# One-hot rows of the gate stage: two VectorE instructions of 512 elements for four tokens in place of four of 128

## The chip, the core and the metric

The kernel runs on 1 core of one Trainium2 chip. The metric is the device time of one execution in microseconds (us), as the median of several runs.

## What is computed

One inference step of a two-layer decoder trunk: 256 prompt tokens and 8 sequences of 4 new tokens, 288 tokens in all, width 1024. Each layer has a mixer (retention with a short convolution in layer 0, HGRN2 in layer 1) and then a PEER channel mixer, which is where the change lies:

```
q = (hb @ wq).reshape(T, PEER_HEADS, 2, PEER_DK // 2)
s = jnp.einsum('thpc,hpkc->thpk', q, keys)
v1, i1 = lax.top_k(s[:, :, 0], PEER_TOPK)
v2, i2 = lax.top_k(s[:, :, 1], PEER_TOPK)
...
eid = e1 * N_KEYS + e2
gate = jax.nn.softmax(vals, axis=-1)
act = jax.nn.gelu(jnp.einsum('thkd,td->thk', u[eid], hb))
w = (gate * act)
return jnp.einsum('thk,thkd->td', w, v[eid])
```

Each token has 8 heads with 16 picks each, 128 picks in all, and each pick names one of 128 x 128 experts by a first index e1 and a second index e2, with a softmax gate. All is float32.

## The kernel before

The kernel doesn't gather experts. For each layer it multiplies all 288 tokens with all 16384 rows of u (section "u0" or "u1", each 128 blocks of 512 KB), keeps the gelu of the products in SBUF (`gates`, 128 partitions x 128 x 288), multiplies that by the gate of each expert, zero for those not picked, and multiplies the result with all rows of v (section "v0" or "v1"). These weight products are split in three passes (lines 1184 to 1186) of a rounded part and its rest, made by ScalarE (line 422) and VectorE (line 660).

Between u and v lies the gate stage, in which the 128 x 128 gate matrix of each token is built as a matrix product over the token's 128 picks. `choice[:, 0, t]` holds the first index of each pick of token t (picks on the partitions), `choice[:, 1, t]` the second one, `choice[:, 2, t]` the gate. For a token, the one-hot row of each pick's first index, scaled by its gate, is one 128 x 128 operand (`onehot`), the one-hot row of its second index the other (`seconds`). Their product over the picks is the gate matrix. Tokens go in groups of four, 6 groups in a turn of the loop (TOKENS = 24), 12 turns and 72 groups in a layer. In each turn:

- VectorE (`weigh`, line 1080) has `firsts` (line 1085), which makes the scaled one-hot rows of a group's tokens, one tensor_scalar a token with compare and multiply (line 1090), into a ring of 8 slots; and `apply` (line 1093), which multiplies the gelus of a group by its gate matrices from PSUM (line 1096). The order written out is firsts 0, firsts 1, apply 0, firsts 2, apply 1, ... firsts 5, apply 4, apply 5, and then the next turn. `firsts` waits until the product that last read the slot is done (`onehot_free`, which TensorE raises for each token), `apply` until its group's four products are done.
- GpSimd (line 367) makes iota minus the second index for a group, 128 x 512, as soon as the slot of two groups before has been read out by ScalarE.
- ScalarE squares it (line 528) and turns it into the one-hot `seconds` by relu(1 - square) (line 531), which waits until the products of two groups before are done.
- TensorE (lines 1399 to 1412) makes the four products of a group into one of two PSUM banks (line 1409). It waits for the bank (`gate_free`, raised by `apply`), for the group's `seconds` (`second_ready`) and, for each token by itself, for its row (`first_ready`). A product of float32 operands is two passes in the profile, so a group has 8.

In layer 0 the loop carries more work: each turn begins with the conditioning products of layer 1 (line 1212, 16 passes of 512 columns), whose weights the SP queue loads into the four `raw` slots; after groups 1 and 3 TensorE turns a part of the result (line 1239), which ScalarE copies before and after (lines 470 and 477), in its own order between the lines 528 and 531.

The order of work on an engine is the order written; nothing is planned at run time.

Of the kernel before, what the change touches and what calls it, by code (L numbers as in the profile page):

```python
# [27 lines left out]
ALU = mybir.AluOpType  # L28
# [3 lines left out]
P = 128  # L32
# [5 lines left out]
T = T_PROMPT + T_SAMPLE  # L38
# [33 lines left out]
TOKENS = 24  # L72
# [29 lines left out]
def trunk(nc, t):  # L102

    with ExitStack() as ctx:
        def sb(name, shape, dt=F32):
            return ctx.enter_context(nc.sbuf_tensor(name, shape, dt))

        def sem(name):
            return ctx.enter_context(nc.semaphore(name))
# [7 lines left out]
        choice = sb("choice", [P, 3, T])  # L117
        onehot = sb("onehot", [P, 8, P])
        ident = sb("ident", [P, P])
        ones = sb("ones", [P, P])  # L120
        iota = sb("iota", [P, P])
# [137 lines left out]
        mixer_done, keys_landed = sem("mixer_done"), sem("keys_landed")  # L259
        x_spilled, x_back = sem("x_spilled"), sem("x_back")  # L260
        exped, picks_ready = sem("exped"), sem("picks_ready")
        first_ready, second_ready = sem("first_ready"), sem("second_ready")
        onehot_free = sem("onehot_free")
        apart_ready, apart_squared = sem("apart_ready"), sem("apart_squared")
        gate_free = sem("gate_free")
# [369 lines left out]
        def _(dve):  # L635
# [444 lines left out]
            def weigh(l):  # L1080

                if l == 0:
                    dve.sem_inc(gate_free, 2)

                def firsts(i, g):

                    for j in range(4):
                        tok = i * TOKENS + (4 * g + j)
                        dve.wait_ge(onehot_free, tok + (T * l + 1))
                        dve.tensor_scalar(onehot[:, (4 * g + j) % 8, :], iota[:], choice[:, 0, bass.ds(tok, 1)], choice[:, 2, bass.ds(tok, 1)],  # L1090
                                          ALU.is_equal, ALU.mult).then_inc(first_ready, 1)

                def apply(i, g):
                    dve.wait_ge(onehot_free, i * TOKENS + (T * l + 4 * g + 4 + 8))
                    w = gates[:, :, bass.ds(i * TOKENS + 4 * g, 4)]
                    dve.tensor_tensor(w, w, ps[:, 6 + g % 2, :].rearrange("p (j e) -> p e j", j=4), ALU.mult).then_inc(gate_free, 1)  # L1096
                with dve.Fori(0, T // TOKENS) as i:
                    firsts(i, 0)
                    for g in range(1, TOKENS // 4):
                        firsts(i, g)  # L1100
                        apply(i, g - 1)
                    apply(i, TOKENS // 4 - 1)
                dve.wait_ge(gate_free, (T // 4) * (l + 1) + 2)
                dve.sem_inc(w_ready, T // 4)  # L1104

# [65 lines left out]
        def _(pe):  # L1171
# [195 lines left out]
            def peer(l):  # L1367
# [12 lines left out]
                for j in range(LISTS):  # L1380
                    g, lo = 32 * (j // 4), (j % 4) * P
# [17 lines left out]
                with pe.Fori(0, T // TOKENS) as i:  # L1399
                    if l == 0:  # L1400
                        pe.wait_ge(ada_row, i * 2 + 24)
                        condition(ps[0:NS, 0, :], i + FIRST["ada1"] // 4)
                    for g in range(TOKENS // 4):
                        pe.wait_ge(gate_free, i * (TOKENS // 4) + ((T // 4) * l + g + 1))
                        for j in range(4):
                            pe.wait_ge(first_ready, i * TOKENS + (T * l + 4 * g + j + 1))
                            if j == 0:
                                pe.wait_ge(second_ready, i * (TOKENS // 4) + (T // 4 * l + g + 1 + 2))
                            pe.matmul(ps[:, 6 + g % 2, j * P:j * P + P], onehot[:, (4 * g + j) % 8, :], seconds[:, g % 2, j, :].bitcast(F32),  # L1409
                                      start=True, stop=True).then_inc(onehot_free, 1)  # L1410
                        if l == 0 and g in (1, 3):
                            turn(i + 12, g // 2)
# [147 lines left out]
```

## Time and profile before

| | us |
|---|---|
| median of 3 runs | 2921.13 (2918.17 to 2921.57) |
| the profiled execution, its span from first to last instruction | 2932.5 |
| TensorE busy in it | 2684.2 |
| VectorE busy in it | 1793.5 |
| ScalarE busy in it | 1351.1 |
| GpSimd busy in it | 181.9 |

The profile is of one execution; the page gives its span and no other time of its own. PE is TensorE's products, PEld its weight loads, DVE VectorE, ACT ScalarE, POOL GpSimd; a name with q (DVEq) is the engine's queue of instructions. Busy time counts an instruction from its start to its end, a hold by another engine included. In a timeline, "x8" means that eight like instructions were merged into one line, and the bracket gives the idle time of the engine before the line and what ended it. PEclk is the mean granted TensorE clock as a share of 2.4 GHz; its two levels are 2.4 and 1.2 GHz.

### The profile page before, as it was taken

What the parts mean: (1) busy time and instruction counts of PE and PEld (TensorE: products, weight loads), DVE (VectorE), ACT (ScalarE), POOL (GpSimd) and SP (SyncE); (2) the same over time, 40 slices, a digit from 0 to 9 for tenths busy, and PEclk for the clock granted to TensorE, in tenths of its full rate; (3) what the DMA queues carried; (4) which work ended last, traced back from release to release, by engine and by line L of the source; (5) the groups of instructions that cost most, each with busy time, mean ns of one, the idle gap of its engine ahead of it and who ended that gap; (6) DMA issues with size and microseconds to landing.
All of it is one profiled execution on the core that took longest, in us unless ns stands there. A gap on an engine that the chain in (4) does not pass through costs nothing.

```text
span 2932.5 us, 55686 instructions
## 1 busy us (share of the span) xinstructions
PE 2684.2 (92%) x17972; PEld 2441.2 (83%) x17972; DVE 1793.5 (61%) x4076; ACT 1351.1 (46%) x2491; POOL 181.9 (6%) x200
## 2 busy tenths in 40 slices
PE   7997899999989899999979796999999866999997
PEld 3962799999955579999979685899999855999996
DVE  2424568884466755555554877589854599555554
ACT  2501345556543445555545323355556544455553
POOL 1000000000022310000000000000000144000000
PEclk8987899999998989999989788899999978999998
DMA  6544444545533335555534112345445300555552
GB/s 231 165 130 161 132 137 158 168 148 163 162 124 100 100 127 182 164 165 164 165 120 162 37 57 102 122 151 161 154 158 165 122 0 0 167 165 165 165 165 86
DMA packets 108380, 401.03 MB, mean 137 GB/s; under 512 B 12352, under 2 KB 12496, under 8 KB 107168
## 3 DMA queue, kind: packets, MB, share of 16 engines
q1 hardware_dynamic: 103104, 375.44, 39.7%
q0 software_dynamic: 5216, 24.87, 2.3%
q8 instruction: 29, 0.48, 0.1%
q14 instruction: 31, 0.25, 0.0%
HBM read 389.60 MB, written 10.65 MB: 136 GB/s over the span
## 4 chain that ended last, share of the span: by engine, by line
PE 81%; DVE 12%; issue 3%; ACT 2%; DMA 1%; DVEq 1%; ACTq 0%; POOL 0%; SPq 0%; POOLq 0%
PE ps L1184 21%; PE ps L1186 21%; PE ps L1185 21%; PE ps L1212 6%; PE ps L1409 4%; DVE onehot L1090 2%; DVE spl L660 1%; PE ps L1329 1%; PE ps L1345 1%; DVE big L1096 1%; PE ps L1358 1%; DMA raw<-in_ada_w 1%; PE ps L1248 1%; DVE big L1041 1%; DVE big L1036 1%
## 5 line engine op out<-in xcount | busy, mean ns | idle before, releaser
L1184 PE MATMUL ps<-hs,spl 128*128 128x288 f32 x4960 | 1481.8, 299 | 75.9 <-DVE hs L712 46.0
L1185 PE MATMUL ps<-hs,spl 128*128 128x288 f32 x4960 | 1473.0, 297 | 0.0
L1186 PE MATMUL ps<-hs,spl 128*128 128x288 f32 x4960 | 1470.5, 296 | 0.0
L660 DVE TENSOR_TENSOR spl<-raw,spl 128x512 fp32r<-128x512 f32 x1240 | 844.4, 692 | 844.9 <-ACT spl L422 842.6
L422 ACT ACTIVATE spl<-raw 128x512 fp32r<-128x512 f32 x1240 | 774.4, 631 | 628.6 <-PE ps L1186 628.2
L1184 PEld LDWEIGHTS ps<-hs,spl 128*128 128x128 f32 x4960 | 940.1, 190 | 89.5 <-issue 58.2
L1186 PEld LDWEIGHTS ps<-hs,spl 128*128 128x128 f32 x4960 | 943.0, 190 | 0.0
L1185 PEld LDWEIGHTS ps<-hs,spl 128*128 128x128 f32 x4960 | 941.7, 190 | 0.0
L1409 PE MATMUL ps<-hs,onehot 128*128 128x128 f32 x1152 | 222.7, 346 | 81.0 <-DVE onehot L1090 56.5
L1409 PEld LDWEIGHTS ps<-hs,onehot 128*128 128x128 f32 x1152 | 185.0, 239 | 121.3 <-issue 56.8
L1090 DVE TENSOR_SCALAR onehot<-iota,choice 128x128 f32<-128x128 f32 x576 | 239.2, 480 | 5.5 <-PEq L1398 4.4
L367 POOL TENSOR_TENSOR hs<-iota,choice 128x512 fp32r<-128x512 f32 x144 | 152.3, 1058 | 1245.7 <-ACT big L517 1002.5
L1212 PE MATMUL ps<-raw,cs 128*10 128x512 f32 x384 | 184.5, 636 | 13.6 <-ACT cs L554 6.7
L517 ACT ACTIVATE big<-ps 128x288 f32 (+1 forms) x256 | 105.6, 412 | 177.9 <-PE ps L1186 177.2
L1212 PEld LDWEIGHTS ps<-raw,cs 128*10 128x10 f32 x384 | 34.7, 96 | 147.2 <-issue 128.5
L1096 DVE TENSOR_TENSOR big<-big,ps 128x512 f32 x144 | 98.0, 681 | 86.7 <-PE ps L1409 85.7
L531 ACT ACTIVATE hs<-hs 128x512 fp32r<-128x512 f32 x144 | 91.0, 632 | 86.6 <-PE ps L1409 78.0
L1123 DVE TENSOR_TENSOR hs<-big,hs 128x288 fp32r<-128x288 f32 x256 | 115.8, 452 | 0.6 <-ACT hs L541 0.6
L541 ACT ACTIVATE hs<-big 128x288 fp32r (+1 forms) x256 | 109.9, 429 | 5.5 <-DVEq L1104 5.5
L517 ACT ACT_TABLE_LOAD x62 | 79.5, 1283 | 63.1 <-PE ps L1186 63.1
L528 ACT ACTIVATE hs<-hs 128x512 fp32r<-128x512 f32 x144 | 88.7, 616 | 3.2 <-POOL hs L367 3.1
L484 ACT ACTIVATE big<-ps 128x288 f32 (+1 forms) x92 | 37.9, 412 | 95.8 <-PE ps L1186 95.7
(222 smaller groups left out, 1292.3 us busy)
## 6 DMA issues: line engine op xcount, KB each, us to landing
raw<-in_peer_u SPq DMA_DIRECT2D x256, 512.0 KB, 3.4
raw<-in_peer_v SPq DMA_DIRECT2D x256, 512.0 KB, 3.4
raw<-in_ada_w SPq DMA_DIRECT2D x96, 512.0 KB, 4.3
raw<-in_peer_wq SPq DMA_DIRECT2D x32, 512.0 KB, 3.3
raw<-in_hg_w_in SPq DMA_DIRECT2D x32, 512.0 KB, 3.4
raw<-in_ab_w_in SPq DMA_DIRECT2D x28, 512.0 KB, 3.4
raw<-in_ab_w_out SPq DMA_DIRECT2D x8, 512.0 KB, 3.9
big<-in_state_hgrn POOLq DMA_DIRECT2D x8, 512.0 KB, 3.9
```

The source lines that it names most:

```text
L367: pool.tensor_tensor(apart[:, g % 2], iota[:, None, :].broadcast_to([P, 4, P]), choice[:, 1, bass.ds(i * TOKENS + 4 * g, 4)][:, :, None].b ...
L422: act.activation(spl[:, slot % 2, 0, cols], raw[:, slot, cols], ACT.Copy).then_inc(high_ready, 1)
L517: act.activation(gates[:, bass.ds(i * 4 + s, 1), :], ps[:, s % 2:s % 2 + 1, 0:T], ACT.Gelu).then_inc(gelu_ready, 1)
L660: dve.tensor_tensor(spl[:, slot % 2, 1, cols], raw[:, slot, cols], spl[:, slot % 2, 0, cols].bitcast(F32), ALU.subtract).then_inc(low_read ...
L1090: dve.tensor_scalar(onehot[:, (4 * g + j) % 8, :], iota[:], choice[:, 0, bass.ds(tok, 1)], choice[:, 2, bass.ds(tok, 1)], ALU.is_equal, AL ...
L1096: dve.tensor_tensor(w, w, ps[:, 6 + g % 2, :].rearrange("p (j e) -> p e j", j=4), ALU.mult).then_inc(gate_free, 1)
L1123: dve.tensor_tensor(hs[:, 1, slot, :], gates[:, bass.ds(e, 1), :].rearrange("p a t -> p (a t)"), hs[:, 0, slot, :].bitcast(F32), ALU.subtr ...
L1184: pe.matmul(out, spl[:, slot, 0, cols], high, start=start, stop=False, skip_group_check=True)
L1185: pe.matmul(out, spl[:, slot, 0, cols], low, start=False, stop=False, skip_group_check=True)
L1186: return pe.matmul(out, spl[:, slot, 1, cols], high, start=False, stop=stop, skip_group_check=True)
L1212: ins = pe.matmul(out, cs[:, k, :], raw[:, k // 2, ROWS * (k % 2):ROWS * (k % 2) + ROWS], start=k == 0, stop=k == KC - 1)
L1409: pe.matmul(ps[:, 6 + g % 2, j * P:j * P + P], onehot[:, (4 * g + j) % 8, :], seconds[:, g % 2, j, :].bitcast(F32), start=True, stop=True) ...
```

## The change

`firsts` is replaced by two functions. `mark` compares iota with the first indices of four tokens, broadcast to 128 x 4 x 128, in one tensor_tensor of 512 elements a partition, and raises a new semaphore `first_marked`. `scale` waits for that and multiplies the four rows in place by the four tokens' gates, also broadcast, in a second tensor_tensor, and raises `first_ready` once for the group. TensorE waits for `first_ready` once for each group, ahead of its first token. `mark` waits until all four slots are free.

The order on VectorE is changed too. A step of group g is scale g, apply g - 1, mark g + 1. At the end of a turn the order is scale 5, apply 4, mark and scale of the next turn's group 0, apply 5, mark of the next turn's group 1. For this the first turn's beginning and the last turn's end are written out, and the loop runs 11 times over what lies between.

```diff
--- before.py
+++ after.py
@@ -259,7 +259,7 @@
         mixer_done, keys_landed = sem("mixer_done"), sem("keys_landed")
         x_spilled, x_back = sem("x_spilled"), sem("x_back")
         exped, picks_ready = sem("exped"), sem("picks_ready")
-        first_ready, second_ready = sem("first_ready"), sem("second_ready")
+        first_marked, first_ready, second_ready = sem("first_marked"), sem("first_ready"), sem("second_ready")
         onehot_free = sem("onehot_free")
         apart_ready, apart_squared = sem("apart_ready"), sem("apart_squared")
         gate_free = sem("gate_free")
@@ -1082,24 +1082,51 @@
                 if l == 0:
                     dve.sem_inc(gate_free, 2)
 
-                def firsts(i, g):
-
-                    for j in range(4):
-                        tok = i * TOKENS + (4 * g + j)
-                        dve.wait_ge(onehot_free, tok + (T * l + 1))
-                        dve.tensor_scalar(onehot[:, (4 * g + j) % 8, :], iota[:], choice[:, 0, bass.ds(tok, 1)], choice[:, 2, bass.ds(tok, 1)],
-                                          ALU.is_equal, ALU.mult).then_inc(first_ready, 1)
+                groups = TOKENS // 4
+
+                def four(g):
+                    return onehot[:, 4 * (g % 2):4 * (g % 2) + 4, :]
+
+                def mark(i, g):
+
+                    dve.wait_ge(onehot_free, i * TOKENS + (T * l + 4 * g + 4))
+                    dve.tensor_tensor(four(g), iota[:, None, :].broadcast_to([P, 4, P]),
+                                      choice[:, 0, bass.ds(i * TOKENS + 4 * g, 4)][:, :, None].broadcast_to([P, 4, P]),
+                                      ALU.is_equal).then_inc(first_marked, 1)
+
+                def scale(i, g):
+
+                    dve.wait_ge(first_marked, i * groups + (T // 4 * l + g + 1))
+                    dve.tensor_tensor(four(g), four(g),
+                                      choice[:, 2, bass.ds(i * TOKENS + 4 * g, 4)][:, :, None].broadcast_to([P, 4, P]),
+                                      ALU.mult).then_inc(first_ready, 1)
 
                 def apply(i, g):
                     dve.wait_ge(onehot_free, i * TOKENS + (T * l + 4 * g + 4 + 8))
                     w = gates[:, :, bass.ds(i * TOKENS + 4 * g, 4)]
                     dve.tensor_tensor(w, w, ps[:, 6 + g % 2, :].rearrange("p (j e) -> p e j", j=4), ALU.mult).then_inc(gate_free, 1)
-                with dve.Fori(0, T // TOKENS) as i:
-                    firsts(i, 0)
-                    for g in range(1, TOKENS // 4):
-                        firsts(i, g)
+
+                def step(i, g, more=True):
+                    scale(i, g)
+                    if g:
                         apply(i, g - 1)
-                    apply(i, TOKENS // 4 - 1)
+                    if more:
+                        mark(i, g + 1)
+                last = T // TOKENS - 1
+                mark(0, 0)
+                for g in range(groups - 1):
+                    step(0, g)
+                with dve.Fori(0, last) as i:
+                    scale(i, groups - 1)
+                    apply(i, groups - 2)
+                    mark(i + 1, 0)
+                    scale(i + 1, 0)
+                    apply(i, groups - 1)
+                    mark(i + 1, 1)
+                    for g in range(1, groups - 1):
+                        step(i + 1, g)
+                step(last, groups - 1, more=False)
+                apply(last, groups - 1)
                 dve.wait_ge(gate_free, (T // 4) * (l + 1) + 2)
                 dve.sem_inc(w_ready, T // 4)
 
@@ -1403,8 +1430,8 @@
                     for g in range(TOKENS // 4):
                         pe.wait_ge(gate_free, i * (TOKENS // 4) + ((T // 4) * l + g + 1))
                         for j in range(4):
-                            pe.wait_ge(first_ready, i * TOKENS + (T * l + 4 * g + j + 1))
                             if j == 0:
+                                pe.wait_ge(first_ready, i * (TOKENS // 4) + (T // 4 * l + g + 1))
                                 pe.wait_ge(second_ready, i * (TOKENS // 4) + (T // 4 * l + g + 1 + 2))
                             pe.matmul(ps[:, 6 + g % 2, j * P:j * P + P], onehot[:, (4 * g + j) % 8, :], seconds[:, g % 2, j, :].bitcast(F32),
                                       start=True, stop=True).then_inc(onehot_free, 1)
```

## Rows read from the trace of the kernel before

**Rows 1.** The page: engines' busy time, and the chain that ended last.

```profile
PE 2684.2 (92%) x17972; PEld 2441.2 (83%) x17972; DVE 1793.5 (61%) x4076; ACT 1351.1 (46%) x2491; POOL 181.9 (6%) x200
...
PE 81%; DVE 12%; issue 3%; ACT 2%; DMA 1%; DVEq 1%; ACTq 0%; POOL 0%; SPq 0%; POOLq 0%
PE ps L1184 21%; PE ps L1186 21%; PE ps L1185 21%; PE ps L1212 6%; PE ps L1409 4%; DVE onehot L1090 2%; DVE spl L660 1%; PE ps L1329 1%; PE ps L1345 1%; DVE big L1096 1%; PE ps L1358 1%; DMA raw<-in_ada_w 1%; PE ps L1248 1%; DVE big L1041 1%; DVE big L1036 1%
```

**Rows 2.** Busy us by stretch, gate stages: PE, PEld, DVE, ACT, POOL, clock, DMA, GB/s.

```profile
824.40:1062.80 238.40, 210.88 (x857) 119.82 (x858) 158.35 (x359) 103.12 (x217) 75.42 (x72) 0.87 0.32 106
2325.90:2492.40 166.50, 112.92 (x576) 96.39 (x576) 161.24 (x360) 83.44 (x144) 76.92 (x72) 0.79 0.00 1
```

**Rows 3.** Groups of instructions, layer 1's gate stage: busy us, mean ns, idle before.

```profile
L1090 DVE TENSOR_SCALAR onehot<-iota,choice 128x128 f32<-128x128 f32 x288 | 120.9, 484 | 1.1 <-ACT big L517 1.1
...
L367 POOL TENSOR_TENSOR hs<-iota,choice 128x512 fp32r<-128x512 f32 x72 | 76.9, 1069 | 585.5 <-ACT big L517 501.4 <-ACT hs L531 84.0
L1096 DVE TENSOR_TENSOR big<-big,ps 128x512 f32 x72 | 49.0, 680 | 5.3 <-PE ps L1409 4.5
```

**Rows 4.** Timeline, the last groups of layer 1, where GpSimd is done.

```profile
2487.17 1.18 PE L1409 MATMUL ps<-hs,onehot 128*128 128x128 f32 x8 [0.39 <-DVE onehot L1090]
...
2488.39 0.63 ACT L531 ACTIVATE hs<-hs 128x512 fp32r<-128x512 f32 x1 [0.42 <-PE ps L1409]
...
2489.34 0.68 DVE L1096 TENSOR_TENSOR big<-big,ps 128x512 f32 x1
2489.94 1.11 DVE L1090 TENSOR_SCALAR onehot<-iota,choice 128x128 f32<-128x128 f32 x4
...
2490.42 1.18 PE L1409 MATMUL ps<-hs,onehot 128*128 128x128 f32 x8 [0.44 <-DVE onehot L1090]
2490.97 1.44 DVE L1096 TENSOR_TENSOR big<-big,ps 128x512 f32 x2
```

**Rows 5.** Timeline, a loop turn's start in layer 1: start, us, engine, line.

```profile
2453.63 2.98 DVE L1090 TENSOR_SCALAR onehot<-iota,choice 128x128 f32<-128x128 f32 x8
2453.70 1.04 POOL L367 TENSOR_TENSOR hs<-iota,choice 128x512 fp32r<-128x512 f32 x1 [1.47 <-ACT hs L531]
...
2454.95 4.74 PE L1409 MATMUL ps<-hs,onehot 128*128 128x128 f32 x24 [2.10 <-DVE onehot L1090]
2456.59 0.63 ACT L531 ACTIVATE hs<-hs 128x512 fp32r<-128x512 f32 x1 [2.54 <-PE ps L1409]
...
2457.28 1.83 DVE L1090 TENSOR_SCALAR onehot<-iota,choice 128x128 f32<-128x128 f32 x4
2457.39 1.13 POOL L367 TENSOR_TENSOR hs<-iota,choice 128x512 fp32r<-128x512 f32 x1 [2.65 <-ACT hs L531]
```

**Rows 6.** Groups by shape, whole span: VectorE tensor_tensor with both inputs in SBUF.

```profile
L660 DVE TENSOR_TENSOR spl<-raw,spl 128x512 fp32r<-128x512 f32 x1240 | 844.4, 692 | 844.9 <-ACT spl L422 842.6
...
L1036 DVE TENSOR_TENSOR big<-big,iota 128x2048 f32<-128x2048 f32 x8 | 18.3, 2289 | 0.1
```

**Rows 7.** Timeline, VectorE: a wait on the instruction right ahead.

```profile
731.80 0.57 DVE L1057 TENSOR_REDUCE small<-rstd 128x8 f32<-128x128 f32 x3
732.40 0.30 DVE L1060 RECIPROCAL small<-small 128x8 f32<-128x8 f32 x3
```

**Rows 8.** Timeline, TensorE in a turn of layer 0: conditioning, groups 0 and 5.

```profile
844.53 7.03 PE L1212 MATMUL ps<-raw,cs 128*10 128x512 f32 x16
851.49 1.16 PE L1409 MATMUL ps<-hs,onehot 128*128 128x128 f32 x8
...
861.74 2.10 PE L1409 MATMUL ps<-hs,onehot 128*128 128x128 f32 x8 [0.56 <-DVE onehot L1090]
```

**Rows 9.** Timeline, VectorE in the same turn: groups 2 and 5.

```profile
853.38 2.67 DVE L1090 TENSOR_SCALAR onehot<-iota,choice 128x128 f32<-128x128 f32 x4
...
861.16 1.83 DVE L1090 TENSOR_SCALAR onehot<-iota,choice 128x128 f32<-128x128 f32 x4
```

## The prediction

> **What bounds the kernel now.** I read the page first: TensorE is busy 92% of the span and the chain that ended last is 81% TensorE, but nearly all of that belongs to the weight products of lines 1184 to 1186 [rows 1]. The gate building of the change is elsewhere: two stretches, the gate stage of layer 0 (238.4 us) and of layer 1 (166.5 us), found by asking when line 1090 runs and then tabulating those stretches [rows 2]. Only they can move. In layer 1 VectorE is busy 161.2 of 166.5 us while TensorE has 112.9: VectorE sets the pace. In layer 0 TensorE is busy 210.9 of 238.4 us, because it also does the conditioning products.
>
> The groups of layer 1 show why VectorE is full [rows 3]: 288 row makers (line 1090) take 484 ns on average, although four with nothing in their way take 1.11 us together, 0.34 for one and a pitch of (1.11 - 0.34) / 3 = 0.257 [rows 4]. The timeline shows the rest [rows 5]. A row maker starts at 2453.63, GpSimd's line 367 at 2453.70; TensorE gets its first row only at 2454.95. A product starts 0.14 after its row is done (2489.94 + 0.34 to 2490.42 [rows 4]), so that row ended at 2454.81, 0.07 after GpSimd's end at 2454.74, and 0.84 late. At 2457.28 the row maker came first by more, and GpSimd took 1.13 in place of 1.04. So the two hold each other off. The product of VectorE with gates (line 1096) runs beside GpSimd unharmed at 680 ns mean [rows 3]; one of its inputs is in PSUM. Besides, at each turn of the loop TensorE stands for 2.10 us [rows 5]: the last product, the last line 1096, then a held row maker, one after the other.
>
> **The change, part by part.** A group is four tokens; a layer has 72, so before costs 166.5 / 72 = 2.31 us each in layer 1.
>
> *Instructions.* Four row makers per group go (4 x 0.257 = 1.03 us of pitch unheld). Two 512-element tensor_tensors come. A 512-element one takes 0.692, a 2048-element one 2.289, both from SBUF [rows 6]: 1.04 ns an element, 0.53 us of streaming and 0.16 around it. I take 0.68 for each, of which 0.12 lies ahead of the streaming and 0.04 behind. When nothing is awaited the next starts 0.60 after (2489.34 to 2489.94 [rows 4]). So VectorE gets more work, not less.
>
> *The new wait.* The scaling waits for the marking right ahead of it on the same engine. Nearest row: a semaphored pair, 731.80 + 0.57 to 732.40 [rows 7], 0.03 after the end; I take 0.04, so 0.72 from one start to the other. Queued behind it are the scaling, line 1096 and the next marking.
>
> *The hand-over.* TensorE now waits for a group's four rows together rather than for each. Its 8 passes take 1.16 at full clock [rows 8] and start 0.14 after the scaling ends.
>
> *The loop's turn.* The marks and scalings of the next turn go ahead of the last line 1096, so the 2.10 us stop goes; what is late next is VectorE's chain below. The first and last turns written out cost instructions only; I cost them at nothing, since VectorE's queue runs ahead of its work; without that cover each turn would pay some queue operations. No DMA is moved and no queue but VectorE's and TensorE's waits changes.
>
> *Does GpSimd hold off the new instructions?* No row shows a tensor_tensor with both inputs in SBUF beside GpSimd. Bounds: never held, as line 1096; or held whole, as line 1090. I take held: the new ones read everything from SBUF, where line 367 reads too, and the row that escapes has an input in PSUM. The Trainium skill (SBUF — State Buffer, section "Who interferes with whom") says that a VectorE instruction with two SBUF inputs contends with a GpSimd instruction that reads SBUF, which speaks against this change. By it the sum below holds; without it the first rival does; no run here shows it yet.
>
> *Sum for layer 1.* I follow one group round. Scaling ends; 0.14; TensorE 1.16; ScalarE's line 531 starts 0.04 later (2487.17 + 1.18 to 2488.39 [rows 4]); GpSimd starts 0.80 after that (2456.59 to 2457.39 [rows 5]); it holds the inputs from about 0.12 for 0.88 (its 1.04 less the same 0.16). Meanwhile line 1096 runs hidden. Marking was issued but is held, streams 0.53, 0.04 to its end, 0.04 wait, 0.12, scaling streams 0.53, 0.04. Sum 0.14 + 1.16 + 0.04 + 0.80 + 0.12 + 0.88 + 1.30 = 4.44 for two groups, since GpSimd works two ahead: **2.22 a group**. At half clock TensorE's 8 passes take 2.10 [rows 8], and the round gives 2.69; where the marking gets in ahead of GpSimd it is about 2.53; I take 2.60. The mean granted clock in this stage was 0.79 [rows 2], so 42% of the time at 1.2 GHz. The long stops after which it stood at half are gone, but no row shows this new rhythm. Ends: none at half, or 42% again; I take the middle, 21%: 2.30. 71 x 2.30 = 163.3, plus a head of 2.5 (GpSimd 1.04, two activations of 0.63, hand-overs) and a tail of 2.1 (0.14 + 1.16 + 0.13 + 0.68, the 0.13 being 2490.42 + 1.18 to the second line 1096 at 2491.73 [rows 4]): 167.9, or **+1.4**. Ends: 162.2 (-4.3) with none, 173.6 (+7.1) with 42%.
>
> *Sum for layer 0.* Each of 12 turns begins with 7.03 us of conditioning products [rows 8], which hide the first two groups before and after: the loop's turn gains nothing. Groups 2 to 5 took VectorE from 853.38 to 861.16 + 1.83 = 862.99, 2.40 each [rows 9]; 4 x (2.40 - 2.30) = 0.4 won. Against it TensorE starts after the fourth row, not the first: 3 x 0.257 = 0.77 lost, where TensorE is not late itself; at 2.10 for the last group [rows 8] it mostly is, and then the loss is hidden. I take +0.1 a turn, **+1** in all, ends -5 and +6.
>
> Together +2.4. The profiled span of 2932.5 is 11.4 above the median 2921.13 of the timed runs (0.4%); both stages are the same work in either, so I carry the difference over as it is: 2923.5.
>
> **Rivals.** *First: GpSimd does not hold them.* For it: line 1096 keeps its 680 ns next to the same GpSimd work. Against it: where its inputs lie. Then VectorE's own chain is the pace: 0.72 + 0.60 + 0.60 = 1.92 a group, 2.18 at half clock (0.14 + 2.10 + 0.13 + 0.60 + 0.72 + 0.68 is 4.37 for two), 1.97 at 21%. Layer 1: 71 x 1.97 + 4.6 = 144.5, -22. Layer 0: 4 x (2.40 - 1.97) - 0.77 = 0.95 a turn, -11. Time 2888; 2880 to 2895 with the clock's ends.
>
> *Second, slower: TensorE at half clock under the group-wise hand-over.* It lies in the round: a product no longer starts on the first row while the others are made, so its whole 2.10 stands in series with GpSimd's hold, and each group at half clock costs 0.38 more. Layer 1 is then above before by more than 0.2% with layer 0's +1 from 2.35 a group, which is 34% at half clock. Before had 42%. At 42% and +4 in layer 0: +11, 2932; at half clock throughout +23 and up to +6: 2950. For it: the clock stood at half for much of a stage that VectorE, not TensorE, paced, as it would again. Against it: the 2.10 us stops are gone.
>
> *Third: it does not relieve VectorE at all,* as 2 x 0.68 against 4 x 0.257 suggests; this is in the forecast's sum, whose gain is only the turn.
>
> **How the numbers follow.** A measurement of this kernel can tell about 0.2%, 5.8 us, from no change. Forecast 0.47 (0.36 within, 0.11 faster, where hand-overs are 0.1 us a group shorter), first rival 0.20, second 0.33: faster 0.31, same 0.36, slower 0.33. The range takes in the first rival to 2880 and the second to 2938 (about 55% at half clock); beyond are some 0.15. The forecast's own range is 2914 to 2933.
>
> **What would show it.** Right: 144 markings and 144 scalings in place of 576 row makers; a good part of them well over 0.69, up to 1.5, where line 367 overlaps; line 367 itself above 1.04; layer 1's stage between 162 and 174; no 2.10 us TensorE stop at each turn; layer 0 within 6 us. First rival: all of them at 0.68 and the stage near 145. Second: granted clock of the stage at 0.79 or below and a stage above 173. The forecast is wrong as reasoned if the new instructions are unheld, or held yet the stage is far from 2.2 to 2.4 a group.

## The result and the profile after

The changed kernel took **2980.78 us** (median of 4 runs, 2978.82 to 2982.93) against 2919.65 for the kernel before beside it (4 runs): a ratio of **1.0204**, 95% interval 1.0188 to 1.0221. It is 61 us slower; the prediction was 2923.5 and its range ended at 2938.

The page of the changed kernel, busy times and the groups that took the place of the row makers:

```profile
PE 2720.9 (91%) x17972; PEld 2483.5 (83%) x17972; DVE 1842.6 (62%) x3788; ACT 1348.6 (45%) x2491; POOL 195.4 (7%) x200
...
L1093 DVE TENSOR_TENSOR onehot<-iota,choice 128x512 f32<-128x512 f32 x144 | 159.3, 1106 | 4.8 <-PEq L1425 4.1
...
L1100 DVE TENSOR_TENSOR onehot<-onehot,choice 128x512 f32<-128x512 f32 x144 | 132.8, 922 | 19.8 <-DVE onehot L1093 3.5
```

Line numbers moved: L1093 is the marking, L1100 the scaling, L1107 the product with gates (1096 before), L1436 TensorE's products (1409), L1239 the conditioning (1212). 144 of each new instruction stand there, at 1.11 and 0.92 us where the prediction took 0.68 for one that nothing holds: GpSimd holds a good part of both, as forecast. In layer 1's stage it is mostly the marking:

```profile
L1093 DVE TENSOR_TENSOR onehot<-iota,choice 128x512 f32<-128x512 f32 x72 | 94.8, 1316 | 0.8 <-ACT big L517 0.8
L367 POOL TENSOR_TENSOR hs<-iota,choice 128x512 fp32r<-128x512 f32 x72 | 80.6, 1120 | 612.6 <-ACT big L517 501.4 <-ACT hs L531 110.8
L1100 DVE TENSOR_TENSOR onehot<-onehot,choice 128x512 f32<-128x512 f32 x72 | 56.9, 791 | 9.9 <-DVE onehot L1093 1.8
```

The time was lost in the two gate stages.

The stretches of the two gate stages, from the first row instruction to the end of the last product with gates, in the columns of [rows 2]:

```profile
816.18:1081.89 265.71, 223.52 (x864) 136.38 (x864) 180.55 (x216) 103.67 (x218) 85.26 (x72) 0.78 0.29 95
2341.88:2542.19 200.31, 147.52 (x576) 126.80 (x576) 189.09 (x216) 83.22 (x145) 80.62 (x72) 0.51 0.00 1
```

The stretch of layer 0 in [rows 2] stops 2.7 us short of that end; cut alike, the kernel before has

```profile
824.48:1065.49 241.01, 212.75 (x864) 121.39 (x864) 159.54 (x360) 103.94 (x218) 75.42 (x72) 0.87 0.32 105
```

So layer 0 went from 241.0 to 265.7 (+24.7) and layer 1 from 166.5 to 200.3 (+33.8): 58.5 of the 61 us. (The two profiled executions lie only 47.8 us apart in span, because the one of the kernel before ran 8.3 us longer ahead of its first gate stage, 824.48 against 816.18, where nothing was changed.) Two columns show how the layers differ. In layer 1 the granted clock fell from 0.79 to 0.51: TensorE ran at 1.2 GHz nearly all through the stage. In layer 0 it fell from 0.87 to 0.78. All later stage times are cut in this way.

The timeline of the changed kernel in the middle of layer 1 shows the new round:

```profile
2421.36 2.07 PE L1436 MATMUL ps<-hs,onehot 128*128 128x128 f32 x8 [0.81 <-ACT hs L531]
...
2423.47 0.63 ACT L531 ACTIVATE hs<-hs 128x512 fp32r<-128x512 f32 x1 [1.74 <-PE ps L1436]
2423.74 0.68 DVE L1107 TENSOR_TENSOR big<-big,ps 128x512 f32 x1
...
2424.10 2.07 PE L1436 MATMUL ps<-hs,onehot 128*128 128x128 f32 x8 [0.67 <-ACT hs L531]
2424.27 1.04 POOL L367 TENSOR_TENSOR hs<-iota,choice 128x512 fp32r<-128x512 f32 x1 [1.85 <-ACT hs L531]
2424.34 1.52 DVE L1093 TENSOR_TENSOR onehot<-iota,choice 128x512 f32<-128x512 f32 x1
2426.01 0.69 DVE L1100 TENSOR_TENSOR onehot<-onehot,choice 128x512 f32<-128x512 f32 x1
...
2426.94 2.07 PE L1436 MATMUL ps<-hs,onehot 128*128 128x128 f32 x8 [0.77 <-ACT hs L531]
```

Follow it from the end of the products at 2423.43. Line 531 starts 0.04 later, GpSimd 0.80 after that and ends at 2425.31; the marking, issued 0.07 behind GpSimd, ends at 2425.86, 0.55 after it; the scaling starts 0.15 later, ends at 2426.70, and the products start 0.24 after that. With their 2.07 the round is 3.51 + 2.07 = 5.58 us for two groups, **2.79 each**. It is the chain that the prediction wrote down, with TensorE at half clock on every pass. (The bracket names line 531 as what released the products. That line ends at or shortly before the same moment: the one that starts at 2423.47 makes the operand of a later group. The scaling's end comes 0.23 to 0.28 before 70 of the stage's 72 starts.) The stop of 2.10 us at each turn is gone.

Layer 0 is told best by the third group of a turn. The changed kernel:

```profile
913.10 1.16 PE L1436 MATMUL ps<-hs,onehot 128*128 128x128 f32 x8 [0.63 <-ACT hs L531]
913.22 1.04 POOL L367 TENSOR_TENSOR hs<-iota,choice 128x512 fp32r<-128x512 f32 x1 [9.10 <-ACT hs L531]
913.31 1.50 DVE L1093 TENSOR_TENSOR onehot<-iota,choice 128x512 f32<-128x512 f32 x1
...
914.48 1.22 POOL L367 TENSOR_TENSOR hs<-iota,choice 128x512 fp32r<-128x512 f32 x1 [0.22 <-ACT hs L531]
914.95 1.30 DVE L1100 TENSOR_TENSOR onehot<-onehot,choice 128x512 f32<-128x512 f32 x1
...
916.49 2.07 PE L1436 MATMUL ps<-hs,onehot 128*128 128x128 f32 x8 [1.69 <-DVE onehot L1100]
...
919.13 2.07 PE L1436 MATMUL ps<-hs,onehot 128*128 128x128 f32 x8 [0.57 <-DVE onehot L1100]
```

and TensorE in the kernel before at the same place, in the turn of [rows 8, 9]:

```profile
853.29 1.16 PE L1409 MATMUL ps<-hs,onehot 128*128 128x128 f32 x8 [0.64 <-ACT hs L531]
...
854.91 0.71 PE L1409 MATMUL ps<-hs,onehot 128*128 128x128 f32 x4
...
855.85 0.74 PE L1409 MATMUL ps<-hs,onehot 128*128 128x128 f32 x4 [0.22 <-DVE onehot L1090]
...
857.27 0.94 PE L1409 MATMUL ps<-hs,onehot 128*128 128x128 f32 x6 [0.68 <-ACT hs L531]
```

From the start of the second group's products to the start of the fourth's, before took 857.27 - 853.29 = 3.98, after 919.13 - 913.10 = 6.03: 2.05 more. Two GpSimd instructions come one right after the other here; one holds the marking, the other the scaling, and TensorE stands idle for 1.69. A whole turn went from 19.98 us ((1044.27 - 824.45) / 11 between the starts of the conditioning products) to 22.06 ((1059.15 - 816.53) / 11): 2.1 us, as much as was lost in this place. It is a wait and not the clock: in this turn the third group's products run at half clock (2.07), in every second turn at full clock (1.15), and the fourth group's start 6.03 or 6.04 after the second's in all turns but the first.

### The profile page after: what moved, and what is told of

Its sections match the earlier page's. It is cut to its first block, busy times and chain, and to the rows that moved or that the text cites. A ratio compares the mean times of both kernels' runs of the same rounds, so it can differ in the third digit from the quotient of the medians.

```text
span 2980.3 us, 54323 instructions
## 1 busy us (share of the span) xinstructions
PE 2720.9 (91%) x17972; PEld 2483.5 (83%) x17972; DVE 1842.6 (62%) x3788; ACT 1348.6 (45%) x2491; POOL 195.4 (7%) x200
## 4 chain that ended last, share of the span: by engine, by line
PE 82%; DVE 12%; issue 3%; ACT 2%; DMA 1%; DVEq 0%; ACTq 0%; POOL 0%; SPq 0%; POOLq 0%
PE ps L1211 21%; PE ps L1213 21%; PE ps L1212 21%; PE ps L1436 6%; PE ps L1239 6%; DVE onehot L1093 2%; DVE spl L660 1%; DVE onehot L1100 1%; PE ps L1356 1%; ACT hs L531 1%; PE ps L1372 1%; PE ps L1385 1%; DVE big L1041 1%; PE ps L1275 1%; DVE big L1107 1%
## 5 line engine op out<-in xcount | busy, mean ns | idle before, releaser
L1436 PE MATMUL ps<-hs,onehot 128*128 128x128 f32 x1152 | 266.9, 404 | 93.6 <-ACT hs L531 46.5
L1436 PEld LDWEIGHTS ps<-hs,onehot 128*128 128x128 f32 x1152 | 228.9, 295 | 134.7 <-ACT hs L531 76.0
L367 POOL TENSOR_TENSOR hs<-iota,choice 128x512 fp32r<-128x512 f32 x144 | 165.9, 1153 | 1285.5 <-ACT big L517 1002.9
L1239 PE MATMUL ps<-raw,cs 128*10 128x512 f32 x384 | 178.0, 618 | 12.4 <-ACT cs L554 6.7
L517 ACT ACTIVATE big<-ps 128x288 f32 (+1 forms) x256 | 105.4, 412 | 178.1 <-PE ps L1213 177.5
L1093 DVE TENSOR_TENSOR onehot<-iota,choice 128x512 f32<-128x512 f32 x144 | 159.3, 1106 | 4.8 <-PEq L1425 4.1
L1239 PEld LDWEIGHTS ps<-raw,cs 128*10 128x10 f32 x384 | 34.2, 94 | 139.5 <-issue 122.4
L1107 DVE TENSOR_TENSOR big<-big,ps 128x512 f32 (+1 forms) x144 | 97.9, 680 | 76.5 <-PE ps L1436 76.0
L1100 DVE TENSOR_TENSOR onehot<-onehot,choice 128x512 f32<-128x512 f32 x144 | 132.8, 922 | 19.8 <-DVE onehot L1093 3.5
```

The costliest lines, as they stand in the source:

```text
L367: pool.tensor_tensor(apart[:, g % 2], iota[:, None, :].broadcast_to([P, 4, P]), choice[:, 1, bass.ds(i * TOKENS + 4 * g, 4)][:, :, None].b ...
L517: act.activation(gates[:, bass.ds(i * 4 + s, 1), :], ps[:, s % 2:s % 2 + 1, 0:T], ACT.Gelu).then_inc(gelu_ready, 1)
L1093: dve.tensor_tensor(four(g), iota[:, None, :].broadcast_to([P, 4, P]), choice[:, 0, bass.ds(i * TOKENS + 4 * g, 4)][:, :, None].broadcast_ ...
L1100: dve.tensor_tensor(four(g), four(g), choice[:, 2, bass.ds(i * TOKENS + 4 * g, 4)][:, :, None].broadcast_to([P, 4, P]), ALU.mult).then_inc ...
L1239: ins = pe.matmul(out, cs[:, k, :], raw[:, k // 2, ROWS * (k % 2):ROWS * (k % 2) + ROWS], start=k == 0, stop=k == KC - 1)
```

## The experiments

Three theories were on record. **T1**: GpSimd holds the new instructions, and TensorE's half clock stretches the round in which that hold lies. **T2**: it is the two new waits (scaling on marking, TensorE on the whole group), not the hold. **T3**: the even rhythm of the new order keeps the clock low. All runs in one table; stage times in us, the clock beside them. Each ratio is to runs of the kernel before beside that run (medians 2919.38 to 2922.53):

| run | total | ratio to before, 95% | layer 0 | layer 1 |
|---|---|---|---|---|
| before | 2919.65 | | 241.0, 0.87 | 166.5, 0.79 |
| after | 2980.78 | 1.0188 to 1.0221 | 265.7, 0.78 | 200.3, 0.51 |
| small_after | 2900.26 | 0.9909 to 0.9959 | 229.0, 0.92 | 154.8, 0.85 |
| small_before | 2861.68 | 0.9777 to 0.9834 | 223.0, 0.92 | 122.7, 0.96 |
| psum_after | 2895.00 | 0.9899 to 0.9948 | 223.8, 0.94 | 154.0, 0.84 |
| order_only | 2905.44 | 0.9927 to 0.9985 | 237.4, 0.90 | 151.5, 0.86 |
| order_group | 2947.79 | 1.0066 to 1.0119 | 260.1, 0.79 | 168.4, 0.71 |
| swap_only | 2986.22 | 1.0202 to 1.0262 | 246.6, 0.83 | 217.0, 0.57 |
| warm_after | 2947.52 | 1.0066 to 1.0117 | 264.8, 0.78 | 170.5, 0.99 |
| warm2_group | 2916.62 | 0.9963 to 0.9999 | 244.9, 0.92 | 152.2, 0.98 |
| warm2_after | 2968.38 | 1.0121 to 1.0179 | 283.0, 0.80 | 170.5, 0.99 |
| early_after | 2958.67 | 1.0098 to 1.0158 | 246.6, 0.83 | 192.8, 0.51 |
| early_mid | 2923.88 | 0.9990 to 1.0025 | 245.7, 0.85 | 162.8, 0.80 |
| early_order | 2903.42 | 0.9913 to 0.9958 | 226.5, 0.95 | 162.1, 0.76 |
| psum_order | 2879.18 | 0.9843 to 0.9881 | 223.1, 0.92 | 136.5, 0.99 |
| warm0_psum | 2879.17 | 0.9828 to 0.9873 | 222.8, 1.00 | 136.6, 0.99 |

### What the hold is worth

**small_after** and **small_before** shrink GpSimd's instruction to one element a token, in the changed kernel and in the one before. The second one-hot rows are then not made; everything else runs. Besides the hold, this takes most of GpSimd's own time out of the round (a mean of 0.22 to 0.35 us in place of 1.05 to 1.19). The cuts of code from here on are shortened.

```diff
-pool.tensor_tensor(apart[:, g % 2], iota[:, None, :].broadcast_to([P, 4, P]), ...
+pool.tensor_tensor(apart[:, g % 2, :, 0:1], iota[:, None, 0:1].broadcast_to([P, 4, 1]), ...
-act.activation(apart[:, g % 2], ..., ACT.Square)
+act.activation(apart[:, g % 2], ..., ACT.Relu)
```

> The changed kernel, but GpSimd subtracts 4 elements a group in place of 512 (so the second one-hot rows are not the reference's, and ScalarE's squaring is a relu of the same size). Theory 1 (GpSimd holds the new instructions, and TensorE's half clock stretches the round): markings and scalings fall to 0.68 to 0.70 us each, layer 1's gate stage from 200 to about 165 us if TensorE stays at half clock (0.24 + 2.07 + 0.13 + 0.60 + 0.72 + 0.69 = 4.45 for two groups) and to about 145 if the clock comes back; total 2900 to 2930. Theory 2 (the loss lies in the two new waits, scaling on marking and TensorE on the whole group, not in the hold): the stage stays above 185 and the total above 2965.

> The kernel before with the same small GpSimd subtraction. Theory 1: the row makers fall from 484 ns to 340, layer 1's stage from 166 to about 140 (72 x 1.63 and 12 turns with a stop of under 2 us), total 2880 to 2900, so that hold-free the old instructions are still the faster ones. Theory 2: the hold was never what cost time before, the stage stays at 160 or more.

Marking and scaling fell to 685 and 692 ns in layer 1, the row makers of before from 484 [rows 3] to 343. The hold is worth 2980.8 - 2900.3 = 81 us to the changed kernel and 2919.7 - 2861.7 = 58 to the one before. So GpSimd explains 22.5 of the 61 us; with almost no work on it the change still costs 38.6, of which 32 lie in layer 1 (154.8 against 122.7). The clock of the changed kernel's layer 1 rose as well, from 0.51 to 0.85, so the 81 hold a part of what the clock is worth below. small_after met T1's ranges, and small_before came out 18 us below its own; T2's 185 and 2965 were far off. Neither T1 nor T2 is the whole.

**psum_after** takes the hold away with all work in place: one input of each new instruction comes from PSUM, out of banks that stand empty in this stage.

```diff
+dve.tensor_copy(ps[:, 2, 0:P], iota[:])
+link(dve.tensor_copy(ps[:, 3, 0:T], choice[:, 2, :]))
-dve.tensor_tensor(four(g), iota[:, None, :].broadcast_to([P, 4, P]),
+dve.tensor_tensor(four(g), ps[:, 2:3, 0:P].broadcast_to([P, 4, P]),
...
-                  choice[:, 2, bass.ds(i * TOKENS + 4 * g, 4)][:, :, None]...
+                  ps[:, 3, bass.ds(i * TOKENS + 4 * g, 4)][:, :, None]...
```

> The changed kernel with one operand of each new instruction in PSUM: iota is copied to a free bank and the marking reads it there, the gates are copied to another and the scaling reads them there. GpSimd does its whole subtraction. Theory 1: as with line 1096, neither is held: 0.67 to 0.70 us each, GpSimd's line back to 1.04 us, layer 1's stage 145 to 160 us, total 2895 to 2905, as with the small GpSimd subtraction. If the hold does not depend on where the operands lie: markings and scalings stay at 0.8 to 1.3 us and the total above 2960.

Groups of this run in layer 1's stage (busy us, mean ns):

```profile
L367 POOL TENSOR_TENSOR hs<-iota,choice 128x512 fp32r<-128x512 f32 x72 | 74.8, 1039 | 573.1 <-ACT big L517 501.4 <-ACT hs L531 71.7
L1102 DVE TENSOR_TENSOR onehot<-onehot,ps 128x512 f32<-128x512 f32 x72 | 49.5, 688 | 9.9 <-DVE onehot L1095 1.8
L1095 DVE TENSOR_TENSOR onehot<-ps,choice 128x512 f32<-128x512 f32 x72 | 49.2, 684 | 0.0
```

VectorE and GpSimd no longer touch each other: 684 and 688 ns, GpSimd 1039, total 2895.0, 86 us below the changed kernel and below the one before. The Trainium skill (SBUF — State Buffer, section "Who interferes with whom") says that a VectorE instruction with at most one SBUF input, outside its two-port modes, does not contend with GpSimd, and that one with two contends with a GpSimd instruction that reads SBUF; these rows agree on both sides (1316 and 791 ns in the changed kernel's layer 1, where both inputs lie in SBUF).

### Which part of the change costs

**order_only** has only the new order, with the four row makers and a hand-over by tokens. **order_group** adds that TensorE waits once for a group's four rows. **swap_only** has the two instructions and the hand-over by groups, in the old order.

```diff
 # order_only, order_group: before's firsts, in the new order
+with dve.Fori(0, last) as i:
+    firsts(i, end); apply(i, end - 1); firsts(i + 1, 0); apply(i, end)
+    for g in range(1, end): firsts(i + 1, g); apply(i + 1, g - 1)
 # order_group, besides: only the fourth row maker raises first_ready
-pe.wait_ge(first_ready, i * TOKENS + (T * l + 4 * g + j + 1))
+if j == 0: pe.wait_ge(first_ready, i * (TOKENS // 4) + (T // 4 * l + g + 1))
 # swap_only: after's mark and scale, in the old order
+mark(i, g); scale(i, g); apply(i, g - 1)
```

> The kernel before with the changed order of work across the loop's turn, but the old row makers and the old token-wise hand-over. Theory 1: the 2.10 us stop of TensorE at each turn goes, layer 1's stage falls by 5 to 25 us, total 2895 to 2915. Theory 3 (the even rhythm of the new order, not the new instructions, keeps TensorE at half clock): the granted clock of the stage is 0.6 or below and the stage above 180.

> The old row makers in the new order, but TensorE waits for the four rows of a group together, as in the change. If the group-wise hand-over is the step that costs (rival), layer 1's stage goes from 151 us (new order alone) to 175 or more and the clock to 0.6 or below. Theory 1, by which the hold on two long instructions that follow each other is what costs: 151 to 165 us, total 2905 to 2925.

> The two new instructions and the group-wise hand-over, in the old order of the loop. Theory 1: the hold and the long round stay and the turn's stop comes back, so layer 1's stage is 200 or more and the total 2980 to 3010. Theory 3: with the stop back the clock is 0.75 or more and the stage falls to 170 to 185, total 2930 to 2955.

The new order by itself wins 14 us, as T1 has it. The hand-over by groups costs 42 on top of it (22.7 in layer 0, 16.9 in layer 1), a clear miss for T1; the 175 us and the clock of 0.6 of its rival were not reached either (168.4, 0.71). The two instructions in place of four cost 33 more (5.6 and 31.9). T3 falls: the new order with before's instructions has a higher clock than before, 0.86 against 0.79. (And the old order of swap_only stands at 0.57, while its 217.0 and 2986.2 lie in T1's range.) But the terms do not simply add: in layer 0 the instructions and the hand-over together cost 5.6 in the old order (swap_only, 246.6 against 241.0) and 28.3 in the new one (265.7 against order_only's 237.4). The timeline of swap_only at the third group of a turn shows why:

```profile
910.00 1.16 PE L1423 MATMUL ps<-hs,onehot 128*128 128x128 f32 x8 [0.63 <-ACT hs L531]
910.10 0.69 DVE L1093 TENSOR_TENSOR onehot<-iota,choice 128x512 f32<-128x512 f32 x1
910.12 3.00 POOL L367 TENSOR_TENSOR hs<-iota,choice 128x512 fp32r<-128x512 f32 x2 [8.26 <-ACT hs L531]
910.93 1.30 DVE L1100 TENSOR_TENSOR onehot<-onehot,choice 128x512 f32<-128x512 f32 x1
...
912.46 1.15 PE L1423 MATMUL ps<-hs,onehot 128*128 128x128 f32 x8 [0.77 <-DVE onehot L1100]
```

Here the marking comes 0.02 ahead of GpSimd and is not held (0.69); in the changed kernel it comes 0.09 behind and is (1.50). TensorE's stop is 0.77 against 1.69, and the turn 20.47 against 22.06. The 0.11 that separates the two lies in the product with gates ahead: it starts 0.23 after TensorE's end in the changed kernel (911.31 + 1.16 to 912.70), 0.12 in swap_only (908.21 + 1.16 to 909.49). Why is open.

### What the clock is worth

**warm_after** is the changed kernel with three idle products into an unused bank behind each group of layer 1. **warm2_group** puts these into order_group, and two behind the groups 2 to 5 of layer 0; **warm2_after** does the same in the changed kernel.

```diff
 pe.matmul(ps[:, 6 + g % 2, ...], onehot[...], seconds[...], start=True, stop=True).then_inc(onehot_free, 1)
+for j in range(3 if l else 0):      # warm2_*: range(3 if l else 2 * (g > 1))
+    pe.matmul(ps[:, 3, j * P:j * P + P], ident[:], iota[:], start=True, stop=True)
```

> The changed kernel; in layer 1's gate stage TensorE makes three idle products (ident by iota, into a PSUM bank that nobody reads there) behind each group's four. Theory 1: the stage is slow because TensorE's 8 passes take 2.07 us at half clock in a round of 5.58 us for two groups; if the extra products bring the clock to 2.4 GHz, the round is 5.58 - 0.91 = 4.67, 2.33 a group, and layer 1's stage falls from 200 to 170 to 175 us, with the hold still there (markings still at 1.2 to 1.3 us on average). Rival: the clock is only a symptom of a slow round; with it at full the stage stays above 190. If the clock does not rise, the extra passes themselves lengthen the stage above 250 and the run decides nothing.

> The same idle products in the kernel that has the new order and the group-wise hand-over, but the four row makers of before. If the hand-over by groups costs mostly through the clock that it sets off, then layer 1 is 151 to 158 us and layer 0 237 to 245 us, total 2905 to 2918 us. If the later start of the products costs by itself, layer 1 stays at 165 us or more and the total at 2935 us or more.

> The changed kernel with idle products on TensorE: three behind each group's products in layer 1, two behind the second, third and fourth group's in layer 0. If TensorE's half clock is what makes layer 0 long as well, the conditioning there ends earlier: layer 1 stays near 170 us, layer 0 falls from 265 to about 245 us, total about 2930 us. If the clock is not the matter in layer 0, its stage stays at 260 us or more, total 2943 us or more.

The stretch of layer 1 in warm_after, and both in warm2_group:

```profile
2338.88:2509.39 170.51, 132.66 (x1008) 119.48 (x1008) 159.72 (x216) 83.21 (x145) 76.61 (x72) 0.99 0.01 2
```

```profile
816.18:1061.09 244.91, 214.23 (x1056) 136.78 (x1056) 175.00 (x360) 103.71 (x218) 75.72 (x72) 0.92 0.32 103
2319.68:2471.89 152.21, 130.99 (x1008) 120.57 (x1008) 150.08 (x360) 83.02 (x144) 75.33 (x72) 0.98 0.01 2
```

The idle products raised the clock of layer 1 from 0.51 to 0.99, and the stage fell from 200.3 to 170.5: against a loss of 33.8 us, **29.8 come back with the clock** (the kernel before, at 0.79, would gain by a full clock too; that was not run). Two groups of warm_after stand 2.33 apart (products at 2421.98 and 2424.31), which is the round above with TensorE's 1.15. The marking's mean fell to 979 ns, outside the forecast of 1.2 to 1.3 us, but the hold is the same: the marking is issued later against GpSimd and still ends 0.55 after it, in 69 of 72 groups (60 of 72 in the changed kernel). For order_group, the whole price of the hand-over in layer 1 goes with the clock (168.4 to 152.2, order_only 151.5), and in layer 0 15.2 of 22.7; all three numbers lie where the text puts them if the clock is the cause. So the hand-over by groups costs little by its later start and most by the clock that it sets off. warm2_after decides nothing for layer 0: the clock stayed at 0.80, and the stage grew to 283.0, as the idle products stand in TensorE's order there. (In layer 0 the idle products stand behind four groups of a turn, not three as the text says; so it is in warm2_group and in warm0_psum below.)

### Does it matter who comes first?

The two instructions and the hand-over stay, but a group's row instructions go ahead of the product with gates behind which they stood, so that the product is that of two groups before. **early_after**: marking, scaling, product; **early_mid**: marking, product, scaling; **early_order**: the same with before's row makers.

```diff
 # all: the first two groups ahead, then for each group g, the turns written out as before
-scale(i, g); apply(i, g - 1); mark(i, g + 1)
+mark(i, g); scale(i, g); apply(i, g - 2)      # early_after
+mark(i, g); apply(i, g - 2); scale(i, g)      # early_mid
+firsts(i, g); apply(i, g - 2)                 # early_order
```

> The changed kernel's two instructions and its hand-over by groups, but on VectorE the marking and the scaling of a group go ahead of the product with gates for which they waited until now, so that they are issued 0.8 us earlier against GpSimd. If the loss comes from the new instructions reaching their inputs after GpSimd does, the marking now comes first and is unheld, VectorE's own 1.9 to 2.0 us a group set the pace and layer 1 is 138 to 152 us, layer 0 222 to 240 us, the total 2885 to 2915 us. If two instructions with a wait between and a hand-over by groups cost by themselves, whoever comes first, layer 1 stays at 185 us or more and the total at 2950 us or more.

> As early_after, but with the product with gates between the marking and the scaling: the marking still comes ahead of GpSimd, the scaling behind it. If arrival decides, the marking is near 0.69 us and the scaling is held in its place, and layer 1 lies between early_after and the changed kernel: 142 to 172 us, total 2895 to 2935 us. If arrival does not matter, it is as early_after.

> The kernel before with its four row makers and its hand-over by tokens, the row makers of a group put ahead of the product with gates in the same way. If arrival decides, the row makers mostly run ahead of GpSimd, near 0.26 to 0.35 us each, VectorE needs 1.63 us a group and layer 1 is 120 to 142 us, layer 0 222 to 235 us, total 2862 to 2890 us. If not, layer 1 stays near the 151.5 us of order_only and the total at 2895 us or more.

Layer 1's groups in early_after, then in early_mid:

```profile
L1100 DVE TENSOR_TENSOR onehot<-onehot,choice 128x512 f32<-128x512 f32 x72 | 92.5, 1285 | 9.7
L367 POOL TENSOR_TENSOR hs<-iota,choice 128x512 fp32r<-128x512 f32 x72 | 80.2, 1114 | 605.6 <-ACT big L517 501.6 <-ACT hs L531 103.6
L1093 DVE TENSOR_TENSOR onehot<-iota,choice 128x512 f32<-128x512 f32 x72 | 51.2, 711 | 1.1 <-ACT big L517 0.8 <-PE ps L1433 0.3
```

```profile
L1100 DVE TENSOR_TENSOR onehot<-onehot,choice 128x512 f32<-128x512 f32 x72 | 69.0, 959 | 0.1
L1093 DVE TENSOR_TENSOR onehot<-iota,choice 128x512 f32<-128x512 f32 x72 | 54.8, 761 | 5.2 <-PE ps L1433 4.1 <-ACT big L517 0.8
L1107 DVE TENSOR_TENSOR big<-big,ps 128x512 f32 (+1 forms) x72 | 48.7, 676 | 0.9 <-PE ps L1433 0.9
```

early_after missed its forecasts, in layer 1 with 192.8 against 138 to 152 us, in layer 0 with 246.6 against 222 to 240. The marking did come first and was free (711), but the hold only moved to the scaling (1285), and as the product with gates now waits behind it, TensorE waits for its bank (40.2 us in layer 1). In layer 0, where the lost race was the loss, it won against the changed kernel's 265.7, as swap_only did. early_mid fits its ranges: the product with gates, which nothing holds, fills the time that GpSimd takes, the scaling drops to 959, layer 1 to 162.8 at a clock of 0.80, and the total to that of before (0.9990 to 1.0025): 57 us of the loss come back **by order alone**. early_order met its forecast in layer 0 (226.5) and missed in layer 1 (162.1, worse than order_only's 151.5): its row makers were held as before (484 ns mean, 454 in order_only), and TensorE waited 42.9 us for its bank, for which it did not wait in order_only. So being first did not remove the hold here; a cover for it did.

How sharp the race is can be counted. In the six runs with both new instructions on SBUF and GpSimd's whole instruction, all 73 markings and scalings that start up to 0.2 us ahead of a GpSimd instruction took under 0.75 us, and all 92 that start 0.03 to 0.2 behind one were held. The row makers of before needed a longer lead: those that start 0.01 to 0.03 ahead of GpSimd were all held, those 0.11 to 0.2 ahead never.

### A version that beats both

**psum_order** is order_only with the index row read from PSUM; **warm0_psum** adds two idle products behind the groups 2 to 5 of layer 0.

```diff
+dve.tensor_copy(ps[:, 2, 0:P], iota[:])
-dve.tensor_scalar(onehot[:, (4 * g + j) % 8, :], iota[:], choice...
+dve.tensor_scalar(onehot[:, (4 * g + j) % 8, :], ps[:, 2, 0:P], choice...
```

> The old row makers in the new order, reading iota from PSUM. Theory 1: no hold on them either, and 0.34 us each if the engine's rate is the same from PSUM, so layer 1's stage 125 to 140 us and the total 2860 to 2885, below both kernels; if PSUM makes them slower (0.40 us and more), 2885 to 2900. If they are still held: 2905 as with the new order alone.

> The kernel with the new order, four row makers that read the index row from PSUM and a hand-over by tokens, with two idle products behind the second, third and fourth group's products in layer 0. If TensorE's clock still costs time in layer 0, that stage falls from 223 to about 215 us, total 2865 to 2880 us. If the idle products are only in the way, total 2880 us or more.

The two stages of psum_order, and its row makers in layer 1:

```profile
816.98:1040.09 223.11, 192.70 (x864) 111.11 (x864) 138.68 (x360) 103.69 (x218) 74.78 (x72) 0.92 0.35 113
2301.38:2437.89 136.51, 98.86 (x576) 82.87 (x576) 135.19 (x360) 83.06 (x144) 74.78 (x72) 0.99 0.00 2
```

```profile
L1092 DVE TENSOR_SCALAR onehot<-ps,choice 128x128 f32<-128x128 f32 x288 | 98.6, 412 | 0.0
L367 POOL TENSOR_TENSOR hs<-iota,choice 128x512 fp32r<-128x512 f32 x72 | 74.8, 1039 | 556.9 <-ACT big L517 501.6 <-ACT hs L531 55.4
```

2879.18 us, 1.4% below before and 3.4% below the change, in the ranges given for free row makers, though one takes 0.41 us and not 0.34. A row maker is dearer from PSUM than a free one from SBUF (four in 1.38 us against 1.11 in [rows 4]), but never held, and layer 1's clock is 0.99 without any idle product. Against psum_after, where nothing is held either, it is 15.8 us faster, and its layer 1 17.5: the two instructions and the hand-over by groups cost that much without any hold (with a clock of 0.84 there against 0.99). warm0_psum raised layer 0's clock from 0.92 to 1.00 and won nothing (222.8 against 223.1; 2879.17): a miss. Either the clock no longer costs there or the idle products took up what it gave; that was not separated.

## Why the prediction was wrong

- *Held or not.* Right. Marking and scaling at 1316 and 791 ns mean in layer 1, GpSimd at 1120 (1069 in [rows 3]), the 2.10 us stop gone; psum_after shows what the first rival would have given, 154.0 for layer 1 (144.5 predicted) and 223.8 for layer 0.
- *The round of layer 1.* Right in its steps, short in two of them: hand-over 0.24, not 0.14; marking to scaling mostly 0.15, not 0.04. That is 0.11 a group: 2.33 at full clock (2.22 predicted), 2.79 at half (2.69). warm_after's 170.5 lies 8.3 above the 162.2 given for no half clock, and 71 x 0.11 is 7.8.
- *The clock's share: the first step that failed.* "The long stops after which it stood at half are gone, but no row shows this new rhythm. Ends: none at half, or 42% again; I take the middle, 21%: 2.30." Measured: a granted clock of 0.50 in each stretch of 20 us that was read between 2350 and 2530, so nearly 100%. The upper end was not an end: nothing in the profile kept the share below that of before, and the second rival itself had named the reason. TensorE does its work in one burst of 2.07 and then stands, mostly 0.57 to 0.87, for the scaling. Full clock is worth 29.8 us, of which the sum had 5.7 (167.9 - 162.2); so this step is 24.1 of the 32.4 us by which layer 1 missed its 167.9, and the round's 8.3 are the rest. Why the clock stays at half in this rhythm stays open.
- *Layer 0: the second.* TensorE loses 0.77 a group "where TensorE is not late itself; at 2.10 for the last group [rows 8] it mostly is, and then the loss is hidden. I take +0.1 a turn, **+1** in all, ends -5 and +6." Measured +2.1 a turn, +24.7. The 0.77 was worked out from free row makers, but the third group's rows are held, by two GpSimd instructions one after the other, and TensorE starts behind both instead of on the first row. And the cover was none: TensorE was said to be late, so that its wait would hide, but the 2.05 lost at that group stand in the turn in full. The new order has a part in it, for which the sum had no term: it puts the marking behind GpSimd, and with the old one (swap_only) layer 0 lost only 5.6.
- *The second rival* had the mechanism and the sign, at a chance of 0.33. Its dearest price was 2950 (+23 in layer 1, +6 in layer 0); measured were +33.8 and +24.7. The 23 was short by the 7.8 of the two hand-overs and by some 3 us more (it took 2.60 a group in place of 2.69, for markings ahead of GpSimd, but 61 of 72 were held); the 6 was the other step again.
- *First and last turns written out.* Right that they cost nothing that shows: order_only, which has them too, is 14 us faster than before.

Shown are the hold, the clock in layer 1 and in order_group, and the effect of who comes first in layer 0. That layer 0's loss in the changed kernel is a wait and not the clock is read from its turns; a run of the changed kernel with a full clock there was not had.

## What to carry to other kernels

When a change hands over a whole group where single rows went before, follow the first product of the group, with all holds in it, and price the receiving engine's half clock at its full share as one end of the range. Idle time on the engine that sets a stage's end was not hidden here by that engine being late. And where two engines hold each other off over SBUF, moving one operand of the hot instruction to PSUM, or putting work that reads PSUM under the hold, won time here (26 us from order_only to psum_order, 57 from the changed kernel to early_mid), while fewer and longer instructions by themselves cost 33 (order_group to the changed kernel).

## What the runs showed of the hardware that was not expected

- TensorE stood at 1.2 GHz for nearly all of a 200 us stage, working 2.07 us at a time with stops of mostly 0.57 to 0.87 between; before, with stops of 2.10 at the turns, the granted clock was 0.79, and in psum_order, with 1.37 us of work and stops of 0.51, 0.99. So the clock fell although the long stops were gone.
- An instruction of VectorE that waits for the one right ahead of it mostly starts 0.14 to 0.16 after its end, and TensorE's product that waits for a group's rows mostly 0.24 after their end, whether GpSimd holds or not: 2381.56 to 2381.70 and 2380.36 to 2380.59 in psum_after, where nothing is held.
- A difference of 0.11 us in arrival (0.02 ahead of GpSimd or 0.09 behind) went with 1.6 us in each turn of layer 0, and an operand in PSUM took the race away altogether: of the instructions of psum_after and psum_order that read one, none was held by GpSimd (marking and scaling 684 and 688 ns mean, row makers 412 in layer 1).
